# A 2x2 block identity for 28 of the 40 projection units of the last block

## The reference, cut to what matters

```
proj = h @ w_in                              # (256, 1024) @ (1024, 10240)
qkv  = proj[..., :9216].reshape(B, S, 3, 3, 16, 64)   # q, k, v; three groups; 16 heads of 64
gate = proj[..., 9216:]
q, k = rotary(rms_norm(q)), rotary(rms_norm(k))
o, lse = dilated_window_attention(...) for each of the 3 groups (window, dilation)
o = softmax-over-groups(lse) weighted sum of the three o
x = x + (o * silu(gate)) @ w_out
```

## Time and profile before

| | |
|---|---|
| runs, us | 2334.46, 2335.07, 2339.91 (median 2335.07) |
| span of the profiled execution, us | 2331.6 |
| its own time as a run | not among the three runs; the median is 3.5 us above the span |
| PE busy | 2269.8 us, 97% |
| DVE busy | 881.6 us, 38% |
| ACT busy | 463.2 us, 20% |
| last layer: first projection matmul to the end | 1928.49 to 2331.6 us |
| of it, projection of quad 0 and its norms, until the first scores | 1928.49 to 2006.63 us |
| three quads of attention with the next quad's projection | 2006.63 to 2275.9 us, 89.6 us each |

### The profile page before, as it was taken

How to read it: one execution, slowest core, us unless ns; L and a number is a source line. 1 busy time by engine, 2 the same in 40 slices (tenths; PEclk the granted TensorE clock), 3 DMA queues, 4 the chain that set the end, 5 groups by cost and what they waited for, 6 DMA issues and landing times.

```text
span 2331.6 us, 49885 instructions
## 1 busy us (share of the span) xinstructions
PE 2269.8 (97%) x22220; PEld 1801.6 (77%) x22220; DVE 881.6 (38%) x1903; ACT 463.2 (20%) x853; POOL 27.2 (1%) x66
## 2 busy tenths in 40 slices
PE   8999999999999999989999999999999999999998
PEld 6888767777688877677777777877778868888884
DVE  3675642665434562322022021121123442343443
ACT  2333312000125332110000000000003341232232
POOL 2000000000000000000000000000000000000000
PEclk9999999999999999999999999999999999999999
DMA  9553255777433324549999999999963324333320
GB/s 390 200 199 128 105 220 191 278 293 276 170 140 131 133 103 145 217 180 401 402 401 401 395 402 401 403 405 404 408 254 127 109 91 156 118 124 127 109 73 19
DMA packets 75532, 538.06 MB, mean 231 GB/s; under 512 B 8552, under 2 KB 8560, under 8 KB 11440
## 3 DMA queue, kind: packets, MB, share of 16 engines
q1 hardware_dynamic: 72864, 526.14, 58.1%
q0 software_dynamic: 1360, 4.85, 0.6%
q10 hardware_dynamic: 1088, 3.81, 0.4%
HBM read 529.90 MB, written 4.85 MB: 229 GB/s over the span
## 4 chain that ended last, share of the span: by engine, by line
PE 93%; DVE 3%; ACT 2%; issue 1%; DMA 0%; DVEq 0%; ACTq 0%; SPq 0%
PE ps L901 20%; PE ps L476 17%; PE ps L432 15%; PE ps L443 11%; PE ps L925 7%; PE ps L933 4%; PE ps L744 4%; PE ps L855 3%; PE ps L519 2%; PE ps L769 2%; PE ps L1084 2%; PE ps L1038 1%; PE ps L1054 1%; ACT ring L1419 1%; DVE ring L1796 1%
## 5 line engine op out<-in xcount | busy, mean ns | idle before, releaser
L901 PEld LDWEIGHTS ps<-hT,ring 128*64 128x64 f32 x11264 | 474.8, 138 | 45.9 <-issue 41.3
L901 PE MATMUL ps<-hT,ring 128*64 128x96 f32 x11264 | 485.7, 247 | 6.9 <-DVEq L2480 4.4
L476 PE MATMUL ps<-ring,hT 128*128 128x256 f32 x1792 | 401.0, 380 | 2.7 <-DVE hT L1796 2.1
L476 PEld LDWEIGHTS ps<-ring,hT 128*128 128x128 f32 x1792 | 335.5, 190 | 52.3 <-issue 5.0
L432 PE MATMUL ps<-ring,hT 128*128 128x256 f32 x1664 | 366.0, 380 | 0.0
L432 PEld LDWEIGHTS ps<-ring,hT 128*128 128x128 f32 x1664 | 314.1, 190 | 44.6 <-issue 2.5
L1419 ACT ACTIVATE RA<-ps 128x192 f32<-128x192 f32 (+2 forms) x159 | 69.9, 440 | 1120.7 <-PE ps L901 586.8
L1796 DVE TENSOR_TENSOR RA<-ps,RA 128x192 f32<-128x192 f32 (+1 forms) x99 | 39.1, 395 | 635.8 <-PE ps L901 552.4
L443 PE MATMUL ps<-hT,ring 128*128 128x256 f32 (+1 forms) x1280 | 269.0, 370 | 0.1
L443 PEld LDWEIGHTS ps<-hT,ring 128*128 128x128 f32 x1280 | 232.0, 190 | 33.1 <-issue 3.1
L925 PE MATMUL ps<-ring,RA 128*64 128x512 f32 x704 | 168.0, 594 | 0.2 <-issue 0.2
(11 more groups left out here) (301 smaller groups left out, 1719.1 us busy)
## 6 DMA issues: line engine op xcount, KB each, us to landing
ring<-stream SPq DMA_DIRECT2D x497, 1024.0 KB, 8.9
slots_scratch<-YT ACTq DMA_DIRECT2D x7, 384.0 KB, 8.1
x_rows<-x SPq DMA_DIRECT2D x2, 512.0 KB, 13.5
gates_row<-bgate SPq DMA_DIRECT2D x1, 1024.0 KB, 19.0
QT<-bgate SPq DMA_DIRECT2D x1, 1024.0 KB, 21.0
rows_scratch<-RB ACTq DMA_DIRECT2D x2, 512.0 KB, 4.5
out<-x_rows SPq DMA_DIRECT2D x2, 512.0 KB, 2.7
rowt<-rows SPq DMA_DIRECT2D x1, 460.0 KB, 16.0
```

The lines of the kernel that those rows point to most:

```text
L476: m = pe.matmul(ps[:, b, t * UC:(t + 1) * UC], hT[:, k, t * P:(t + 1) * P], ring[:, s, k * UC:(k + 1) * UC], start=k == 0, stop=k == KC - 1)
L901: m = pe.matmul(ps[64 * j:64 * (j + 1), b, c * CAP:(c + 1) * CAP], ring[:, s, k * UC + c * P + 64 * j:k * UC + c * P + 64 * (j + 1)], hT[: ...
```

## The change

28 of the 40 units are taken in seven sets of four. A set is a block of weights 1024 x 1024, seen as 2 x 2 blocks of 512 (width) x 512 (columns): s11, s12 (upper half of the width, two column blocks), s21, s22. The tokens' side is 2 x 2 too: two token tiles by two halves of the width. Instead of eight products of blocks there are seven, each 4 matmuls of 128x128 by 128x512; sums of token blocks (`token_sums`, once) and of weight blocks (`weight_sums` and `last_sum`, for each set) are made on DVE. Four of the seven results are copied out of PSUM by ACT and three are added to them by DVE (`SUMMED`). Every product takes a bank "U" of its own.

A unit in memory is now a half of the width by 512 columns. Quad 0 has one set (in `dsw`), quads 1 to 3 have two sets each (A and B below; products A0 to A6, B0 to B6); the rest (v2 and gate, and in quad 0 also the first block pair) is projected by 8 matmuls of 512 columns a tile. The steps of a quad (`DSW_STEPS`) hold 3, 3, 3, 3, 2 products and then the two token tiles of v2 and gate: 8, 4 and 4 matmuls. `gate_silu` now runs at n = 7, on the rows in SBUF. The ring has six slots in this layer; the seventh, a row of masks and a gate row hold the weight sums.

```diff
+RING_DSW = 6
+WC = 2 * UC
+KH = KC // 2
-DSW_ORDER = (0, 1, 2, 3, 4, 5, 9, 6, 7, 8)
-DSW_HALVES = [[(DSW_ORDER[i // T], i % T) for i in range(*at)] for at in
-              ((0, 3), (3, 6), (6, 9), (9, 12), (12, 14), (14, 16), (16, 18), (18, 20))]
+DSW_STEPS = [[(0, 0), (0, 1), (0, 2)], [(0, 3), (0, 4), (0, 5)], [(0, 6), (1, 0), (1, 1)],
+             [(1, 2), (1, 3), (1, 4)], [(1, 5), (1, 6)], [("wide", 0, 0), ("wide", 0, 1)],
+             [("wide", 1, 0)], [("wide", 1, 1)]]
+DSW_BLOCKS = ((0, 1), (3, 2))
+DSW_WIDE = 4
+SUMMED = ("act", "dve", "act", "act", "dve", "dve", "act")
+UNIT_ENDS = (2, 4, 5, 6)
...
+            def summed_product(key, i):
+                if i == 0:
+                    u = state["unit"]
+                    state["unit"] += 4
+                    ticket["units", key] = [plan[u + j] for j in range(4)]
+                units = ticket["units", key]
+                s11, _, s22, s21 = (u[0] for u in units)
+                b = next_bank("U")
+                if i in (0, 1):
+                    s, fill, _ = units[0 if i == 0 else 3]
+                    pe.wait_ge(landed[s], 16 * fill)
+                if i in (2, 6):
+                    pe.wait_ge(*sums.more())
...
+                for k in range(KH):
...
+                    m = pe.matmul(ps[:, b, :], lhs, rhs, start=k == 0 and i in (0, 1, 3),
+                                  stop=k == KH - 1, skip_group_check=i not in (0, 1, 3))
...
             def dsw():
-                lead_units("ndsw", [("act", ("dsw", 0, j)) for j in range(2)], order=(1, 0))
-                for j in DSW_ORDER[2:]:
-                    rows_unit("act", ("dsw", 0, j))
+                at = [(landed_unit(), landed_unit()) for _ in range(2)]
...
+                for i in range(len(SUMMED)):
+                    summed_product(("dsw", 0, 1), i)
+                for t in range(T):
+                    for kh in range(2):
+                        wide_half(("dsw", 0, "wide"), t, kh, t == T - 1)
...
             (ScalarE, attention)
                         if not last_one:
                             if n == NORM_STEP:
+                                if groups > 1:
+                                    items_out(qd + 1, n)
                                 root_table()
                                 root(meansq[:, 0:16 * groups])
-                                if (gate, 1) not in halves[n]:
-                                    exp_table()
+                                exp_table()
                             if n == TURN_STEP:
-                                turned(qd + 1)
-                            for j, t_ in halves[n]:
-                                if t_ and j != gate:
-                                    quad_unit(name, qd + 1, j, gate)
+                                turned(qd + 1, 0)
+                            if groups == 1 or n != NORM_STEP:
+                                items_out(qd + 1, n)
+                            if n == TURN_STEP and groups > 1:
+                                turned(qd + 1, 1)
+                                gate_silu(qd + 1)
+                                exp_table()
...
             (VectorE)
+            def weight_sums(key, before):
+                units = ticket["units", key]
+                for s, fill, _ in units[0:3]:
+                    dve.wait_ge(landed[s], 16 * fill)
+                s11, s12, s22, _ = (u[0] for u in units)
+                if before:
+                    bank_of(dve, (before, 3))
+                for i in range(2):
+                    tt(D_T1[i], unit_half(s12, i), unit_half(s11, i), ALU.subtract)
+                for i in range(2):
+                    tt(D_T2[i], unit_half(s22, i), D_T1[i], ALU.subtract)
+                for i in range(2):
+                    tt(unit_half(s12, i), unit_half(s22, i), unit_half(s12, i), ALU.subtract,
+                       c=sums if i else step)
+            def last_sum(key):
+                s, fill, _ = ticket["units", key][3]
+                dve.wait_ge(landed[s], 16 * fill)
+                for i in range(2):
+                    tt(unit_half(s, i), unit_half(s, i), D_T2[i], ALU.subtract, c=sums if i else step)
+            def summed_in(qd, g, i):
...
+                at = bank_of(dve, (key, i))
+                taken((key, first))
+                a = (RA, RB)[qd % 2][:, t, b * WC:(b + 1) * WC]
+                tt(a, ps[:, at, :], a, ALU.add, c=took)
+                if i == 1:
+                    last_sum(key)
...
                         if n + 1 < len(ATT):
                             score(qd, n + 1)
                         if not last_one:
+                            if items:
+                                items(qd + 1, n)
                             quad_norm(qd + 1, n)
...
+                def items(qd, n):
+                    for it in DSW_STEPS[n]:
+                        if it[0] != "wide" and SUMMED[it[1]] == "dve":
+                            summed_in(qd, *it)
+                    if n == 1:
+                        weight_sums(("dsw", qd, 1), ("dsw", qd, 0))
+                    if n == TURN_STEP and qd < QUADS - 1:
+                        weight_sums(("dsw", qd + 1, 0), ("dsw", qd, 1))
+
+                token_sums()
+                dve.wait_ge(unit_done, spare_free)
+                weight_sums(("dsw", 0, 1), None)
+                squares(0, 0)
+                for i in range(len(SUMMED)):
+                    if SUMMED[i] == "dve":
+                        summed_in(0, 1, i)
+                squares(0, 1)
                 for t in range(T):
                     scaled(0, t)
+                weight_sums(("dsw", 1, 0), ("dsw", 0, 1))
```

More of the change, by code:

```diff
@@ L63, with summed_units, dsw_units @@
 TURN_STEP = 7
+def summed_units(ha, hb):
+    return [(0, ha), (0, hb), (1, hb), (1, ha)]
+def dsw_units(q):
+    first = summed_units(*DSW_BLOCKS[0]) if q else [(kh, b) for b in DSW_BLOCKS[0] for kh in range(2)]
+    return first + summed_units(*DSW_BLOCKS[1]) + [(kh, DSW_WIDE) for kh in range(2)]
 def heads_at(qd):
@@ L143, in ring_plan @@
         at += 1
-    return out
+    return out, last[RING_DSW][2]
 class Count:
@@ new lines, in wide_half @@
+            def wide_half(key, t, kh, last):
+                if (key, "unit", kh) not in ticket:
+                    ticket[key, "unit", kh] = landed_unit()
+                s = ticket[key, "unit", kh]
+                if kh == 0:
+                    ticket[key, "bank"] = next_bank("U")
+                b = ticket[key, "bank"]
+                for k in range(kh * KH, (kh + 1) * KH):
+                    m = pe.matmul(ps[:, b, :], hT[:, k, t * P:(t + 1) * P], unit_k(s, k),
+                                  start=k == 0, stop=k == KC - 1)
+                if last:
+                    m.then_inc(unit_done, 1)
+                    if kh == 0:
+                        done.more()
+                        return
+                    unit_full("act", [b], (key, t))
+                elif kh:
+                    finish(m, "act", [b], (key, t))
@@ L1026, in attention @@
+            def attention(groups, tag, name, steps, qk, val, turn, then=None):
                 at, open_unit, late = [], {}, []
@@ L1071, in half, with item @@
                             unit_full("act", [b], key)
+                def item(qd, it):
+                    if groups == 1:
+                        half(qd, *it)
+                    elif it[0] == "wide":
+                        wide_half((name, qd, "wide"), it[1], it[2], it[1] == T - 1)
+                    else:
+                        summed_product((name, qd, it[0]), it[1])
                 def out_columns(key, blocks):
@@ L1107, in attention @@
                                 turn(qd + 1, 0)
-                            for i, (j, t_) in enumerate(halves[n]):
-                                if n == TURN_STEP and i == 1:
-                                    turn(qd + 1, 1)
-                                half(qd + 1, j, t_)
-                            if n == TURN_STEP and len(halves[n]) == 1:
+                            for it in steps[n]:
+                                item(qd + 1, it)
+                            if n == TURN_STEP:
                                 turn(qd + 1, 1)
@@ L1720, in attention @@
                                 blocks_out((tag, qd, n, kt), PT[n % 2][:, kt, 0:groups, :], groups)
-                        if not last_one and (gate, 1) in halves[n]:
+                        if not last_one and groups == 1 and (gate, 1) in steps[n]:
                             quad_unit(name, qd + 1, gate, gate)
```

142 lines of the change are left out of this document (115 added, 27 removed).

## The result

The changed kernel takes 2395.9 us (median; 2392.1 to 2398.2) against 2334.8 us before it on the same chip: ratio 1.0251, 95% interval 1.0233 to 1.0268. It is slower, as forecast, but by 61 us where +29 was forecast, and 2395.9 lies outside the range of 2346 to 2384. By the profiled spans the difference is 2390.0 - 2331.6 = 58.4 us.

The account below looks back on a forecast made before the run. PE was taken as the bound (93% of the chain). Per quad, waits of 16.0 less 7.6 us saved give +8.4, +25 in three; prologue -2, clock +6: +29 on 2335.1, so 2364 us, range 2346 to 2384 for 8 in 10.

Parts of the forecast that it names:

- five waits a quad: PE waits in steps 2, 3, 4 and at start and end of step 7, 16.0 us a quad in all.
- What PE saves: Fewer matmuls on PE: 7.6 us saved in each of three quads, 4.2 us in quad 0, 27 us in all.
- DVE's sums: Weight sums on DVE at 1.225 us each: six before a set's product 2, two more after product 1.
- Step 2: PE waits 3.9 us before B1 for A6's bank, which ACT copies out behind the exponentials of step 3.
- Steps 3, 4, turn, end of step 7: PE waits before B4, second transposes, the turn and the last transposes of each quad: 2.4, 3.5, 2.8, 3.4 us.
- Prologue: PE turns about 4 us earlier, first scores come 2 us earlier; 2 us gained taken, bounds 4.2 gained and 2 lost.
- The clock: Granted clock may fall to half behind the waits: bounds 0 and 45 us, +6 us taken.
- six falls at 1 us each: Of fifteen waits six bring a clock fall costing 1 us, since ACT or DVE often bounds what follows: +6 us.
- rival 3: Clock falls at almost every wait, twelve falls at 2.5 us on top of +23: 2388 us; chance 0.13.
- Rival 1: All waits are covered and the projection's saved time, 27 us, shows in full: 2308 us; chance 0.05.
- rival 2: Waits hold at step 7 but not in steps 2 to 4, if sums took under 0.6 us: 2329 us; chance 0.09.
- Rival 4: Ring of six slots delivers weights too late; with 3 us in each quad 2373 us; chance 0.07.

Follow-up runs that it names:

- e8: e4 and e6 together on the changed kernel, plus the prologue's SiLU and tables behind the copies of the turned rows; 2315.2 us, ratio 0.9917 to the kernel before.
- e6: Changed kernel with VectorE's three additions counting on a semaphore of their own; 2390.7 us, ratio 1.0238 to the kernel before.
- e7: Changed kernel with weight sums cut to 128 of 1024 columns, 7/8 of them left out; 2361.4 us, ratio 1.012 to the kernel before.
- e3: Changed kernel with the root and the gate's SiLU, with their table loads, behind the copies in steps 4 and 7; 2367.3 us, ratio 1.0117.
- e4: Changed kernel reordered: weight sums earlier, squares a step later, root and SiLU behind copies, gate's product in step 6; 2324.3 us, ratio 0.9952.
- e5: Changed kernel with unread filler matmuls at the eight places where PE waited over 2 us; 2370.4 us, ratio 1.0159 to the kernel before.
- e10: e9 plus six or seven unread filler matmuls in each of its four waits; 2332.3 us, ratio 0.9981 to the kernel before.
- e9: e8 with SiLU and its table changes again ahead of the copies in the prologue and step 7; 2343.0 us, ratio 1.0024.
- e1: Changed kernel with unread filler matmuls meant for most waits, nine of them ahead of B1 instead of B0; 2389.6 us, ratio 1.022.

## Why the prediction was wrong

Right: that PE's saving would be lost to five waits a quad, where they come from and how long they are. By the forecast's steps:

- **What PE saves.** Forecast 7.6 us a quad; measured 6.9 to 7.0 (busy time in e8, and after with the clock taken out). The two prices that it stands on, 0.220 and 0.433 us a record, make 8.1 if they aren't rounded on the way.
- **DVE's sums.** Forecast 1.225 us each; measured 1.225.
- **Step 2.** Size right within half a microsecond (3.9; 4.37), place and cause not. The step read only which engine empties B1's bank; it did not ask at which count the bank of B0 is free. e6 shows both obstacles one behind the other. That the two sizes agree is partly luck: both obstacles end behind the same six sums.
- **Steps 3, 4, turn, end of step 7.** 2.4, 3.5, 2.8, 3.4 forecast; 2.18, 3.75, 3.48, 3.06 measured, and removed in e7 (step 3), e3 (step 4 and end of step 7) and e4 (turn). The turn's is longer because the record that ends it is `result`, which stands on VectorE right behind the scaling. The sum, 16.0, was 16.8.
- **Prologue.** PE came to the turn 3.9 us earlier (2000.21 to 1996.34; 4 forecast). ACT with SiLU and its two tables took back 2.5 of them where the working gave it 2, so the first scores begin 1.4 us earlier (2006.63 to 2005.21), for 2. The loss shows as a wait of PE of 3.11 us, which the working did not name, and the clock fell behind it for 10.2 us; at the end of the first scores 0.8 us are left (17.68 to 16.89).
- **The clock.** This is the step that failed: "I take six falls at 1 us each". Sixteen stretches, 72 us at half rate, cost 33.2 us under a busy PE, 31.6 more than before, for a forecast of 6. Add the waits, 49.8, subtract the work saved: 49.8 - 20.9 + 28.9 = 57.8 us in the quads, -0.8 in the prologue and +2.0 in the last part (clock 0.97 there) make 59.0, against 58.4 by the spans. Without the clock's part the forecast is +23 us and the measurement 58.4 - 31.6 = +26.8.

Both halves of "six falls at 1 us" were too low. The number: the argument that what follows a wait is again bound by another engine doesn't lower how often the clock falls; fifteen of the sixteen waits of 2.2 us and more were followed by it. The price: in these stretches PE is not bound by another engine, it was busy in 67 of the 72 us, and all of that ran at half rate. e5 against the kernel after and e10 against e9 price it in two orders: 25.5 us by the medians (31 without the misplaced filler) for 16 waits, 10.7 us for 4. The Trainium skill's account that the forecast cited ("TensorE: Matmul & The Clock Gate", section "A second HAM failure mode: psum-queue depth-cycling"), of a kernel whose PE pauses between groups of matmuls as it cycles through PSUM banks and whose clock falls again and again, agrees with this trace: sixteen stretches after, one before. That was rival 3, twelve falls at 2.5 us or 30 us in all, 2388 us, and it is what came about; I gave it 0.13.

Rival 1 (all waits covered) and rival 2 (no sums of 0.6 us) didn't come about, but e8 shows that rival 1's mechanism was a matter of order and of the counter: with the same work it gives 2315 us. Rival 4 (the ring delivers late) is out: no PE wait of the quads has a DMA as releaser, and VectorE waited for one once, 5.0 us ahead of its first weight sums in the prologue.

Open: why one wait of 2.2 us is followed by half rate and another isn't. In the kernel after the same wait of 2.18 us ahead of B4 stands in all three quads, and the 3.4 us behind it ran at 0.66, 1.00 and 0.50:

```profile
2059.88:2063.30 3.42, 3.42 (x6) 1.40 (x7) 0.00 (x0) 0.58 (x1) 0.00 (x0) 0.66 0.00 0
2168.76:2172.18 3.42, 3.42 (x8) 1.58 (x9) 0.00 (x0) 0.57 (x1) 0.00 (x0) 1.00 0.02 5
2276.03:2279.45 3.42, 3.42 (x4) 1.45 (x5) 0.00 (x0) 0.53 (x1) 0.00 (x0) 0.50 0.00 0
```

Counted over the prologue and the quads of all twelve profiles: each of the 62 waits of 3.06 us or more was followed by half rate, of the 15 of 2.2 us seven, both of 1.84 and 1.96 us, none of the six of 1.2 to 1.5 us. But the length of one wait isn't all of it: the one stretch of the kernel before began at 2002.43, behind waits of 0.92 and 0.87 us. The same kernel's runs differ in it too: the ten runs of the kernel before beside e1 to e4 took 2336.5 to 2343.2 us where the granted clock was 0.992 or 0.993, and 2330.3 to 2338.2 where it was 0.995 or 0.996. The forecast's two bounding rows could not have told this.

## What to carry to other kernels

Where PE sets the end, a change that shortens its work and lengthens another engine's queue is priced by each place at which PE then waits, and here each such wait of 2 to 4 us counted about one and a half to two times its length: itself and, for each stretch of 3.4 us at half rate behind it, some 1.7 us. From 3 us on the fall came every time. In this kernel it paid to put table changes and side work of an engine behind, not ahead of, the copies that free PSUM banks; where a wait can't be removed, matmuls that nobody reads, placed ahead of it, gave back the clock's part. And when several instructions of one engine count on one semaphore, read the order of the counts and not only who empties the bank: here a bank was empty for 8 us and still not free.

## What the hardware showed that I had not expected

- The half rate, most often for 3.4 us at a time, falls mostly on the work behind a wait and not on the wait (2095.35:2098.83 at 0.96, 2098.83:2102.25 at 0.54), though in six of the sixteen stretches it began up to 1.1 us before PE started again.
- Filler only has to stand in the wait, it needn't fill it: idle remainders of 0.3 to 0.6 us brought no fall in e5.
- VectorE's subtraction of two blocks of 128 x 1024 took 1.225 us with the ring's DMAs at 239 GB/s beside it, as in the earlier trace rows; I had left room for contention.
